# Two norms moved by token halves into their neighbour stages, the last two chunks of a feed-forward summed together, and the next seam reordered

## The chip, the cores and the metric

One NeuronCore of a Trainium2 chip runs the whole program in one launch. Its engines are TensorE (PE in the profile), VectorE (DVE), ScalarE (ACT), GpSimd (POOL) and SyncE (SP, which issues the DMAs). The metric is device time in microseconds, from launch to end. Lower is better.

## The reference

Three different transformer blocks run one after the other on x of 1024 tokens by 1024 channels, all in fp32.

```python
def layer_norm(x, g, b):                   # block 1, after each half
    mu = jnp.mean(xf, axis=-1, keepdims=True)
    var = jnp.mean(jnp.square(xf - mu), axis=-1, keepdims=True)
    y = (xf - mu) * lax.rsqrt(var + LN_EPS)
    return (y * g + b)

def rmsnorm(x, g):                         # block 2, ahead of each half and at its end
    return x * lax.rsqrt(jnp.mean(x * x, axis=-1, keepdims=True) + EPS) * g

# block 1: pool + HGRN mixer, then
h = layer_norm(ALPHA * h + mix, ln1_g, ln1_b)
u = h @ w_up                               # 1024 -> 2 x 2816
a, v = split(conv_b + causal_conv3(u, conv_w))
h = layer_norm(ALPHA * h + (gelu(a) * v) @ w_down, ln2_g, ln2_b)
# block 2: h = rmsnorm(x, norm_mix_g); proj = h @ w_in (q, k, v, ga, gb, forget logits)
#   u = ga * sigmoid(gb), causal depthwise convolution over 31 tokens; attention; w_out
#   x = x + square(relu(rmsnorm(x, norm_ffn_g) @ w_ffn_up)) @ w_ffn_down; rmsnorm(x, norm_final_g)
# block 3: modulated layer norm of x and of a context (256 tokens), projection, spatial gating,
#   mLSTM in both directions, w_out; layer norm; modulated layer norm;
#   x = layer_norm(ALPHA_3 * x + g2 * (square(relu(h @ w1 + b1)) @ w2 + b2))
```

## The kernel before

**Layout.** Channels lie on the 128 partitions, tokens along the free side: an activation is 8 tiles (KT) of 128 channels by 1024 tokens, and most instructions work on 512 tokens, a half (n = 0 or 1). X is the residual, H the input of the next product. Products are made in three passes of single-pass precision (fp32r): each operand is split into a rounded high part and a low rest, and each product is high x high, high x low and low x high, three matmuls of 128x512 with 8 tiles of input, so that a unit (128 output channels, 512 tokens) is 24 matmuls. ScalarE rounds the high part, VectorE subtracts to get the low one.

**Stages.** The program is a row of stages. Each is a block in which every engine has its own list of instructions, in the order in which the code calls them, held together by semaphores; a stage ends on all engines before the next begins. The ones that matter are, with their time in the profile: chain_stage for block 1 (467.4 to 1351.7), layer_norm_stage (to 1387.1), block2_project (to 1625.9), some stages of block 2, chain_stage for block 2 (1951.8 to 2789.2), block3_mixer (to about 3197), chain_stage for block 3.

**chain_stage** does w_out, a norm (A), an up projection, the activation and the down projection. The hidden width is taken in chunks: 22 of 128 pairs of channels in block 1 (E = 21 is the last, E-1 the one before), 16 in the others. up_unit makes one unit, down_half the 8 output tiles of one half for one chunk, and VectorE adds each from psum to X (a drain, L1688 or L1685). down_last, in blocks 2 and 3, adds the last two chunks in psum, so that only one drain per tile is needed. At the end stands the final norm, one per half (B[0], B[1]), and in block 2's chain also the first norm of block 3 for half 0 (F).

**HalfNorm** is a norm for one half, as methods that an engine's list calls: add (seven additions of the 8 tiles, for the mean), mean (a matmul with a matrix of 1/1024, which sums over partitions), centre, squares (ScalarE), pairs (four additions of two squares), sums (four matmuls), root (1/sqrt as exp of log on ScalarE), scale (VectorE), apply (ScalarE, with gain and bias) and low (VectorE). Which engine does add and pairs is set where they are called. For a centred norm whose result feeds a product ("split" or "next"), a tile goes through

```python
dve.tensor_tensor(work(k), work(k), rstd, mult)                 # scale, L944
act.activation(hi, work(k), Identity, scale=g(k), bias=b(k))    # L996: the high part, rounded
act.activation(work(k), work(k), Identity, scale=g(k), bias=b(k))   # L998: the full value
dve.tensor_tensor(HR, work(k), hi, subtract)                    # low, L955
```

**layer_norm_stage** between block 1 and block 2 is a whole stage: squares on ScalarE (L467), 16 sum matmuls (L452), root, scale with gain (L504), rounding (L487), low part (L512), for both halves, and the residual is stored to memory (spill), since its buffer is used otherwise in block 2.

**block2_project** takes 11 slabs of weights: 8 for the gates, q and k, a small one, and two for v. Units go slab by slab, in each both halves. For each of the first four slabs VectorE makes u = ga * sigmoid(gb) (gated, L2050) and 31 convolution taps (L2059, L2062), with the splits of later weight slabs (L2043) put between them.

**block3_mixer** begins with the rest of the norms of the second seam: B1 (block 2's final norm, half 1: root and scale L946), F0 and F1 (block 3's first norm), then the units for gates, q and k, the context's scaling (L3083), and rows of the gates (L2839, L2859 to L2870, L3089 on).

## Time and profile before

| | us |
|---|---|
| median of 3 runs (lowest, highest) | 4078.4 (4076.28, 4080.22) |
| profiled execution | 4078.99 |
| its span | 4077.0 |
| TensorE busy | 3735.3 (92%) |
| VectorE busy | 2271.2 (56%) |
| ScalarE busy | 1278.5 (31%) |
| GpSimd busy | 191.3 (5%) |
| mean granted clock of TensorE | 0.959 |

Of the 40 slices of the page, TensorE's busy share falls to 8 and 5 tenths in the two slices from 1223 to 1427, and below 9 in a dozen others. A matmul's length in the timeline is longer than the distance to the next, since they overlap in the array.

### The profile page before, as it was taken

Reading aid. Unit: us, or ns where it says so; the run is one execution under the profiler, and the core shown is the slowest. Engines: PE = TensorE matmul, PEld = TensorE weight load, DVE = VectorE, ACT = ScalarE, POOL = GpSimd, SP = SyncE. Lnnn points to the kernel's source line nnn. Section 1 sums busy time; section 2 is a strip of 40 time slices with the busy share of each in tenths; the row PEclk is TensorE's granted clock in tenths of the full one; section 3 lists DMA queues with packets and bytes.
Section 4 is the critical chain, followed back from the end, with each engine's and each line's share of the span. In section 5 each row is a group of like instructions: output and inputs, shape, how many; then the busy total and the mean of one; then the engine's idle time right before and its main releaser. Section 6 shows DMA issues by size and latency. Waiting matters only on the chain. (4 is left out here: it accounts for less than half of the span.)

```text
span 4077.0 us, 44926 instructions
## 1 busy us (share of the span) xinstructions
PE 3735.3 (92%) x17850; PEld 3048.8 (75%) x17850; DVE 2271.2 (56%) x3220; ACT 1278.5 (31%) x1870; POOL 191.3 (5%) x119
## 2 busy tenths in 40 slices
PE   6987899999998599688899999997898989999997
PEld 5887777888886388366778888885886757888886
DVE  1077667777777597244445645545537574444445
ACT  1142352222222421544332223224422363322323
POOL 3410000000000000000000000003001000000000
PEclk9999899999999799788999999998999999999999
DMA  2110001111110111100112222212122201111111
GB/s 106 51 63 0 21 32 57 47 47 47 47 47 21 72 47 42 62 0 0 42 52 104 93 96 97 97 42 78 36 66 65 76 28 52 42 42 62 42 52 52
DMA packets 60837, 216.56 MB, mean 53 GB/s; under 512 B 4542, under 2 KB 17086, under 8 KB 55155
## 3 DMA queue, kind: packets, MB, share of 16 engines
q1 hardware_dynamic: 60082, 213.37, 14.7%
q8 instruction: 124, 2.03, 0.2%
q10 hardware_dynamic: 576, 0.72, 0.0%
q14 instruction: 55, 0.44, 0.0%
HBM read 200.34 MB, written 13.70 MB: 52 GB/s over the span
## 5 line engine op out<-in xcount | busy, mean ns | idle before, releaser
L1250 PE MATMUL psum<-mixer_r,pairs_r 128*128 128x512 f32 x2016 | 797.9, 396 | 36.0 <-DVE gemm_input_r L1618 19.4
L1251 PE MATMUL psum<-gemm_input_r,pairs_r 128*128 128x512 f32 x2016 | 789.3, 392 | 0.0
L1252 PE MATMUL psum<-mixer_r,pairs_r 128*128 128x512 f32 x2016 | 789.1, 391 | 0.0
L1288 PE MATMUL psum<-hidden_r,pairs_r 128*128 128x512 f32 x1248 | 493.6, 396 | 20.7 <-DVE residual L1688 9.6
L1290 PE MATMUL psum<-hidden_r,pairs_r 128*128 128x512 f32 x1248 | 489.4, 392 | 0.0
L1289 PE MATMUL psum<-hidden_r,pairs_r 128*128 128x512 f32 x1248 | 489.4, 392 | 0.0
L1250 PEld LDWEIGHTS psum<-mixer_r,pairs_r 128*128 128x128 f32 x2016 | 381.3, 189 | 128.1 <-DVE pairs_r L1613 20.6
L1688 DVE TENSOR_TENSOR residual<-residual,psum 128x512 f32<-128x512 f32 x576 | 372.5, 684 | 166.9 <-PE psum L1290 146.5
L1251 PEld LDWEIGHTS psum<-gemm_input_r,pairs_r 128*128 128x128 f32 x2016 | 381.5, 189 | 80.7 <-issue 3.1
L1252 PEld LDWEIGHTS psum<-mixer_r,pairs_r 128*128 128x128 f32 x2016 | 381.1, 189 | 79.6
L1624 DVE TENSOR_TENSOR pairs_r<-pairs,pairs_r 128x2048 fp32r<-128x2048 f32 (+1 forms) x108 | 223.5, 2072 | 279.5 <-ACT pairs_r L1416 279.4
L1416 ACT ACTIVATE pairs_r<-pairs 128x2048 fp32r<-128x2048 f32 (+1 forms) x108 | 187.1, 1736 | 600.1 <-DMA pairs<-in_w 376.1
L1288 PEld LDWEIGHTS psum<-hidden_r,pairs_r 128*128 128x128 f32 x1248 | 236.3, 189 | 73.4 <-DVE residual L1688 10.9
L1685 DVE SCALAR_TENSOR_TENSOR residual<-psum,ada,residual 128x512 f32<-128x512 f32 x240 | 179.7, 751 | 177.0 <-PE psum L1290 168.0
L1290 PEld LDWEIGHTS psum<-hidden_r,pairs_r 128*128 128x128 f32 x1248 | 236.3, 189 | 49.7
L1289 PEld LDWEIGHTS psum<-hidden_r,pairs_r 128*128 128x128 f32 x1248 | 236.6, 190 | 49.1 <-issue 0.8
L1648 DVE TENSOR_TENSOR hidden_r<-mixer,hidden_r 128x512 fp32r<-128x512 f32 x172 | 118.8, 691 | 107.2 <-ACT mixer L1433 87.3
L1424 ACT ACTIVATE conv_raw<-psum 128x512 f32<-128x512 f32 x88 | 52.4, 597 | 353.9 <-PE psum L1252 353.9
L2062 DVE SCALAR_TENSOR_TENSOR mixer<-scratch,params,mixer 128x1024 f32<-128x1024 f32 x120 | 154.1, 1284 | 3.9
L1657 DVE TENSOR_SCALAR mixer<-conv_raw,params 128x512 f32<-128x512 f32 x88 | 48.1, 546 | 158.6 <-ACT conv_raw L1424 158.6
L247 PE MATMUL psum<-gemm_input_r,weights_r 128*128 128x512 f32 x256 | 100.6, 393 | 34.6 <-DVE residual_r L614 34.6
L1972 PE MATMUL psum<-residual_r,pairs_r 128*128 128x512 f32 x272 | 107.1, 394 | 23.5 <-DVE pairs_r L2043 23.5
(470 smaller groups left out, 5937.1 us busy)
## 6 DMA issues: line engine op xcount, KB each, us to landing
pairs<-in_w_up SPq DMA_DIRECT2D x38, 1024.0 KB, 7.1
pairs<-in_w SPq DMA_DIRECT2D x32, 1024.0 KB, 5.3
pairs<-in_w_down SPq DMA_DIRECT2D x16, 1024.0 KB, 5.2
norm_a<-in_w_ada SPq DMA_DIRECT2D x12, 1024.0 KB, 5.1
norm_b<-in_w_ada SPq DMA_DIRECT2D x12, 1024.0 KB, 5.0
pairs<-in_w_down SPq DMA_DIRECT2D x22, 512.0 KB, 3.3
pairs<-in_w_in SPq DMA_DIRECT2D x11, 1024.0 KB, 5.2
weight_slots<-in_w_in SPq DMA_DIRECT2D x10, 1024.0 KB, 4.8
```

Of the source, the lines that this page charges most:

```text
L1250: pe.matmul(out, w_hi[:, at], c.MR[:, k, halves[n]], start=k == 0, stop=False)
L1251: pe.matmul(out, w_hi[:, at], c.HR[:, k, halves[n]], start=False, stop=False)
L1252: mm = pe.matmul(out, w_lo[:, at], c.MR[:, k, halves[n]], start=False, stop=k == KT - 1)
L1288: pe.matmul(bank, hi, hid(0, ch, n, kd), start=kd == 0, stop=False)
L1289: pe.matmul(bank, lo, hid(0, ch, n, kd), start=False, stop=False)
L1290: mm = pe.matmul(bank, hi, hid(1, ch, n, kd), start=False, stop=kd == KD - 1)
L1416: act.activation(hi, src, ACT.Copy).then_inc(split_hi, 1)
L1624: dve.tensor_tensor(lo, src, hi.bitcast(F32), ALU.subtract).then_inc(split_ready, 1)
L1648: dve.tensor_tensor(hid(1, ch, n, m), mixed[n][:, m, :], hid(0, ch, n, m).bitcast(F32), ALU.subtract).then_inc(hid_ready, 1)
L1685: dve.scalar_tensor_tensor(out=x, in0=ps, scalar=gate(m), in1=x, op0=ALU.mult, op1=ALU.add).then_inc(down_drained, 1)
L1688: dve.tensor_tensor(x, x, ps, ALU.add).then_inc(down_drained, 1)
L2062: dve.scalar_tensor_tensor(out=out, in0=U[:, j:j + T], scalar=w, in1=out, op0=ALU.mult, op1=ALU.add).then_inc(taps, 1)
```

## The change

**First seam.** layer_norm_stage between block 1 and block 2 is gone. Its norm (norm_2) is two HalfNorms now. For half 0, its squares and three of its pair sums are at the end of block 1's chain (F), and its last pair sum, sums, root, scale, apply and low are at the start of block2_project (F0). The final norm of block 1 is split too: half 0 (B[0]) in the chain, half 1 (B1) with its adds in the chain and all else in block2_project, followed by F1. All adds and pair sums of these four are on GpSimd. block2_project takes the first three slabs for half 0 first (six units), then for half 1, and from the fourth on both halves slab by slab. Three slabs are loaded in the chain. The residual is stored in four parts, by half and by four tiles.

**Last chunks of block 1.** The order (E-1,0), (E-1,1), (E,0), (E,1) becomes (E-1,0), (E,0), (E-1,1), (E,1), and the down sums of the two chunks are one psum sum with one drain per tile.

**Second seam.** The mixer's gate slab is rounded and split in the chain before. F's sums come two tiles earlier. B[1]'s mean and sums leave the chain (norm_final is not centred, so only the sums count); B1's last pair sum and sums open the mixer. B1's root stands between F0's rounding of tiles 0 to 2 and the rest. B1's eight final scales come behind slab q's split. F1's sums come before slab k's second unit. The eight context scalings go from VectorE (L3083) to ScalarE.

**HalfNorm.** For centred norms of kind "split" or "next" (lean), the gain goes into scale and the bias into the rounding and into low. The activation L998 is gone for them. This holds for block 3's norm at the second seam and for the second norm of block 3's chain.

```diff
@@ HalfNorm @@
+        self.lean = self.centred and self.kind in ("split", "next")
...
-        if self.centred:
+        if self.centred and not self.lean:
             dve.tensor_tensor(self.work(k), self.work(k), self.rstd, ALU.mult).then_inc(self.s["scaled"], 1)
         else:
-            dve.scalar_tensor_tensor(out=self.work(k), in0=self.x(k), scalar=self.g(k), in1=self.rstd, op0=ALU.mult,
-                                     op1=ALU.mult).then_inc(self.s["scaled"], 1)
+            dve.scalar_tensor_tensor(out=self.work(k), in0=self.work(k) if self.centred else self.x(k), scalar=self.g(k),
+                                     in1=self.rstd, op0=ALU.mult, op1=ALU.mult).then_inc(self.s["scaled"], 1)
...
+        if self.lean:
+            dve.scalar_tensor_tensor(out=self.c.HR[:, k, self.half], in0=self.work(k), scalar=self.b(k),
+                                     in1=self.hi(k).bitcast(F32), op0=ALU.add, op1=ALU.subtract).then_inc(self.s["lo_ready"], 1)
+            return
...
+            if self.lean:
+                act.activation(hi, self.work(k), ACT.Identity, bias=self.b(k)).then_inc(self.s["hi_ready"], 1)
+                continue
@@ chain_stage, TensorE, block 1 @@
+                up_unit(E, 0, 0)
+                up_unit(E, 0, 1)
+                up_unit(E - 1, 1, 0)
                 down_last(0, range(0, 4))
                 down_last(0, range(4, 8))
-            up_unit(E, 1, 0)
...
+                up_unit(E - 1, 1, 1)
+                B[0].mean(pe)
+                up_unit(E, 1, 0)
+                up_unit(E, 1, 1)
                 B[0].sums(pe)
+                down_last(1, range(0, 4))
+                down_last(1, range(4, 8))
@@ chain_stage, GpSimd, block 1 @@
+                for k in range(1, KT):
+                    B[0].add(pool, k, (down_drained, down_at[E, 0, k]))
+                B[0].pairs(pool)
+                for k in range(1, KT):
+                    B[1].add(pool, k, (down_drained, down_at[E, 1, k]))
+                F.pairs(pool, range(0, 3))
@@ chain_stage, VectorE, block 1, its end @@
+                for k in range(0, 4):
+                    b0.scale(dve, k)
+                for m in range(4):
+                    drain(E, 1, m)
+                    b0.scale(dve, 4 + m)
+                drains(E, 1, range(4, 8))
+                return
@@ block2_project, TensorE @@
-            for i in range(9):
...
+            B1.mean(pe)
+            F0.sums(pe)
+            unit(0, 0, 0, F0.s["lo_ready"])
+            unit(0, 1, 0)
+            unit(1, 0, 0)
+            B1.sums(pe)
+            unit(1, 1, 0)
+            unit(2, 0, 0)
+            unit(2, 1, 0)
+            F1.sums(pe)
+            unit(0, 0, 1, F1.s["lo_ready"])
+            for u in units[7:]:
+                unit(*u)
@@ block2_project, VectorE @@
             split_slab(0)
+            B1.centre(dve, range(0, 4))
+            F0.scale_low(dve, 2)
             split_slab(1)
+            B1.centre(dve, range(4, 8))
+            split_slab(2)
+            for k in range(KT):
+                B1.scale(dve, k)
+            F1.scale_low(dve, 2)
             gated(0)
@@ block3_mixer @@
+            B1.sums(pe)
             unit("gate", 0, 0, F0.s["lo_ready"])
...
             unit("k", 0, 0)
+            F1.sums(pe)
             unit("k", 1, 0)
-            F1.sums(pe)
...
+            for k in range(KT):
+                scale, shift = [c.ada[:, 2 * (i + k) + 1:2 * (i + k) + 2] for i in (8, 0)]
+                act.activation(N[:, k, :], N[:, k, :], ACT.Identity, scale=scale, bias=shift).then_inc(ctx_step, 1)
...
-            F0.scale_low(dve, 3)
+            F0.scale_low(dve, 2)
+            split_slab("q")
             for k in range(KT):
                 B1.scale(dve, k)
-            split_slab("q")
             split_slab("k")
...
-                dve.tensor_scalar(N[:, k, :], N[:, k, :], scale, shift, ALU.mult, ALU.add).then_inc(ctx_step, 1)
@@ plan @@
-            (2, lambda f: layer_norm_stage(c, X, H, KT, ones_d, rms_eps, g("norm_mix_g_2"), centre=False,
-                                           hi=XR, lo=HR, spill=True,
-                                           prefetch=f("w_in_2"))),
-            (2, lambda f: block2_project(c)),
+            (2, lambda f: block2_project(c, final_1, norm_2)),
```

The instruction lists show where the work goes. VectorE at the end of block 1's chain and up to the first split of the projection, before (residual is X, norm_a and norm_b hold sums and squares, a branch ends a stage):

```order
L926 TENSOR_TENSOR norm_a<-norm_a,residual 128x512
L933 TENSOR_TENSOR residual<-residual,psum 128x512 x8
L938 TENSOR_TENSOR norm_a<-norm_a 128x512
L938 TENSOR_TENSOR norm_b<-norm_b 128x512 x3
L944 TENSOR_TENSOR residual<-residual,norm_a 128x512 x8
L136 UNCONDITIONAL_BRANCH
L489 UNCONDITIONAL_BRANCH
L504 SCALAR_TENSOR_TENSOR gemm_input<-residual,params,scratch 128x512 x8
L512 TENSOR_TENSOR gemm_input_r<-gemm_input,residual_r 128x512 x8
L504 SCALAR_TENSOR_TENSOR gemm_input<-residual,params,scratch 128x512 x8
L512 TENSOR_TENSOR gemm_input_r<-gemm_input,residual_r 128x512 x8
```

and now:

```order
L1756 TENSOR_TENSOR residual<-residual,psum 128x512
L955 TENSOR_TENSOR residual<-residual,norm_a 128x512
L1756 TENSOR_TENSOR residual<-residual,psum 128x512 x4
L136 UNCONDITIONAL_BRANCH
L2181 UNCONDITIONAL_BRANCH
L2208 MEMSET scratch 128x30
L2186 TENSOR_TENSOR pairs_r<-pairs,pairs_r 128x2x1024
L944 TENSOR_TENSOR residual<-residual,psum 128x512 x4
L957 SCALAR_TENSOR_TENSOR gemm_input<-residual,params,norm_a 128x512 x3
L970 TENSOR_TENSOR gemm_input_r<-gemm_input,residual_r 128x512
L957 SCALAR_TENSOR_TENSOR gemm_input<-residual,params,norm_a 128x512
```

The adds (L926), the pair sums (L938) and half 1's centre (L933) and scale (L944) have left the stage's end, and the scales and low parts of the norm between stand in the projection. GpSimd had nothing there. Its list at the end of block 1's chain and in the projection is now (L937 is add, L949 pairs):

```order
L1657 UNCONDITIONAL_BRANCH
L937 TENSOR_TENSOR norm_a<-residual 128x512
L937 TENSOR_TENSOR norm_a<-norm_a,residual 128x512 x6
L949 TENSOR_TENSOR norm_a<-norm_a 128x512
L949 TENSOR_TENSOR norm_b<-norm_b 128x512 x3
L937 TENSOR_TENSOR norm_a<-residual 128x512
L937 TENSOR_TENSOR norm_a<-norm_a,residual 128x512 x6
L949 TENSOR_TENSOR norm_a<-norm_a 128x512
L949 TENSOR_TENSOR norm_b<-norm_b 128x512 x2
```

These are B[0]'s adds and pairs, B[1]'s adds and three pairs of F. ScalarE at the start of block 3's mixer, before:

```order
L978 ACT_TABLE_LOAD
L980 ACTIVATE norm_a<-psum,rms_eps 128x512
L982 ACTIVATE norm_a<-norm_a 128x512
L2807 ACTIVATE pairs_r<-pairs 128x1024
L996 ACTIVATE residual_r<-gemm_input,ada 128x512
L998 ACTIVATE gemm_input<-gemm_input,ada 128x512
L996 ACTIVATE residual_r<-gemm_input,ada 128x512
L998 ACTIVATE gemm_input<-gemm_input,ada 128x512
```

and now:

```order
L1011 ACTIVATE residual_r<-gemm_input,ada 128x512 x3
L993 ACT_TABLE_LOAD
L995 ACTIVATE norm_a<-psum,rms_eps 128x512
L997 ACTIVATE norm_a<-norm_a 128x512
L1011 ACTIVATE residual_r<-gemm_input,ada 128x512 x3
L2958 ACTIVATE hidden_r<-mixer 128x2x1024
L1011 ACTIVATE residual_r<-gemm_input,ada 128x512 x2
L2958 ACTIVATE pairs_r<-pairs 128x2x1024
L2990 ACTIVATE rows<-psum,row_params 128x512
L3003 ACTIVATE pairs<-pairs,ada 128x256 x8
```

One activation a tile in place of two, the gate slab's rounding (L2807 with 128x1024) has left the stage, and the context's scalings (L3003) are new here.

## Rows read from the trace of the kernel before

**Rows 1.** The page: the span, and busy time of each engine with its instructions.

```profile
span 4077.0 us, 44926 instructions
...
PE 3735.3 (92%) x17850; PEld 3048.8 (75%) x17850; DVE 2271.2 (56%) x3220; ACT 1278.5 (31%) x1870; POOL 191.3 (5%) x119
```

**Rows 2.** Waits of TensorE, 1255 to 1395: total, times, longest, in us.

```profile
PE psum L1972 <- DVE pairs_r L2043: 23.5, 1, 23.5
PE psum L912 <- DVE norm_a L926: 9.9, 1, 9.9
PE psum L452 <- ACT scratch L467: 9.0, 1, 9.0
PE psum L1288 <- DVE residual L1688: 7.7, 1, 7.7
PE psum L917 <- DVE norm_a L938: 5.6, 1, 5.6
PE psum L1288 <- DVE hidden_r L1648: 3.8, 1, 3.8
```

**Rows 3.** Windows, all engines: length, busy us (instructions), granted clock, DMA share, GB/s.

```profile
1272.10:1391.92 119.82, 60.46 (x174) 36.83 (x173) 81.36 (x128) 54.92 (x84) 0.00 (x0) 0.76 0.13 53
1391.92:1625.50 233.58, 233.52 (x1200) 201.00 (x1200) 186.38 (x141) 48.60 (x65) 0.00 (x0) 0.99 0.11 39
```

**Rows 4.** Timeline, first seam and projection: start, length, engine, line, operation, [idle before].

```profile
1276.00 0.47 PE L1288 MATMUL psum<-hidden_r,pairs_r 128*128 128x512 f32 x1 [3.77 <-DVE hidden_r L1648]
...
1280.88 0.40 PE L1290 MATMUL psum<-hidden_r,pairs_r 128*128 128x512 f32 x1
...
1366.79 0.75 DVE L504 SCALAR_TENSOR_TENSOR gemm_input<-residual,params,scratch 128x512 f32<-128x512 f32 x1 [16.67 <-ACT scratch L474]
...
1372.10 0.68 DVE L512 TENSOR_TENSOR gemm_input_r<-gemm_input,residual_r 128x512 fp32r<-128x512 f32 x1
...
1391.77 0.79 PE L1972 MATMUL psum<-residual_r,pairs_r 128*128 128x512 f32 x1 [23.48 <-DVE pairs_r L2043]
...
1416.84 1.23 DVE L2050 TENSOR_TENSOR scratch<-mixer 128x1024 f32<-128x1024 f32 x1 [22.92 <-ACT mixer L2000]
...
1597.69 1.28 DVE L2062 SCALAR_TENSOR_TENSOR mixer<-scratch,params,mixer 128x1024 f32<-128x1024 f32 x1
```

**Rows 5.** Timeline, second seam.

```profile
2797.50 0.77 PE L2585 MATMUL psum<-residual_r,pairs_r 128*128 128x512 f32 x1 [8.30 <-DVE gemm_input_r L955]
...
2808.15 1.41 DVE L946 SCALAR_TENSOR_TENSOR residual<-residual,params,norm_a 128x512 f32<-128x512 f32 x2
...
2815.79 0.79 PE L2585 MATMUL psum<-residual_r,hidden_r 128*128 128x512 f32 x1 [6.54 <-DVE hidden_r L2961]
...
2845.51 1.89 ACT L2854 ACTIVATE ctx_hi<-pairs 128x2048 fp32r<-128x2048 f32 x1
...
2875.86 1.48 DVE L3089 SCALAR_TENSOR_TENSOR mixer<-mixer 36x1280 f32<-36x1280 f32 x1 [12.62 <-ACT mixer L2870]
```

**Rows 6.** Timeline, GpSimd, and VectorE beside it, second seam.

```profile
2758.79 1.54 POOL L926 TENSOR_TENSOR norm_a<-norm_a,residual 128x512 f32<-128x512 f32 x1
...
2813.45 2.29 DVE L2961 TENSOR_TENSOR hidden_r<-mixer,hidden_r 128x2048 fp32r<-128x2048 f32 x1
...
2813.61 5.46 POOL L926 TENSOR_TENSOR norm_a<-residual 128x512 f32<-128x512 f32 x1 [25.59 <-DVE residual L946]
...
2817.85 1.37 DVE L3083 TENSOR_SCALAR pairs<-pairs,ada 128x256 f32<-128x256 f32 x1
...
2819.22 1.28 POOL L926 TENSOR_TENSOR norm_a<-norm_a,residual 128x512 f32<-128x512 f32 x1
```

**Rows 7.** Timeline, second norm of the third feed-forward, half 1.

```profile
3372.58 0.81 ACT L996 ACTIVATE mixer_r<-gemm_input,ada 128x512 fp32r<-128x512 f32 x1 [0.76 <-DVE gemm_input L944]
...
3373.43 0.81 ACT L998 ACTIVATE gemm_input<-gemm_input,ada 128x512 f32<-128x512 f32 x1
...
3385.15 0.69 DVE L955 TENSOR_TENSOR gemm_input_r<-gemm_input,mixer_r 128x512 fp32r<-128x512 f32 x1 [0.86 <-ACT gemm_input L998]
```

385 lines of the change are left out of this document (241 added, 144 removed).

## The prediction, on record before the changed kernel ran

> **What bounds the kernel now.** I read the page first: TensorE is busy 92% of the span [rows 1], so only stretches in which TensorE waits or runs on other things than products can give much. The profiled execution took 4078.99 us, its span is 4077.0 and 2.0 lie around it; the median of the runs shown is 4078.4, so the sum below is made against 4079.0 and then moved by -0.6. Next the waits of TensorE from 1255 to 1395: six waits, 23.5 + 9.9 + 9.0 + 7.7 + 5.6 + 3.8 = 59.5 us, all on VectorE or ScalarE steps of a norm, a drain or a split [rows 2]. Then the windows: from 1272.10 to 1391.92, 119.8 us long, TensorE is busy 60.5 us with 174 matmuls, at a mean granted clock of 0.76; the projection behind it, 233.6 us, is dense [rows 3]. At full clock one 128x512 product follows the last after 0.227 us (816 x 0.227 and 384 half as wide at 0.127 make the 233.6); behind the wait of 3.77 us at 1276.00 the first thirteen took 4.9 us instead of 2.95, in part 0.43 apart, the 1.2 GHz level [rows 4]. By the code the 119.8 us hold five units of 24 products that are needed anyway (the chunk's down sums for half 0, its two up units for half 1, the down sums of both chunks for half 1): 120 x 0.227 = 27.2 us. The rest, 92.6 us, is seam: norm sums, waits and low clock.
>
> The second seam (second feed-forward to the third block's mixer) has waits of 8.3 and 6.5 us [rows 5], and in the third feed-forward an eight-tile norm is paced by ScalarE [rows 7].
>
> **Seam 1, part by part.** Removed: the stage between, 1351.7 to 1387.1 = 35.4 us. Its sum matmuls (16, recorded as 32; 15.5 us) and its squares, scales and roundings (L504 twice 5.4 us, L512 twice 4.9 us) [rows 4] come back as two half norms of 4 sum matmuls each, since squares are added in pairs first. Of the 16 drains of chunk E-1, 0.61 us apart on VectorE, nothing remains: both chunks add up in one psum bank, so the wait of 7.7 us for a drain and the 3.8 us for hidden_r (filled now by another unit's products) go [rows 2]. The seven adds and four pair sums of a half, now between drains on VectorE (0.69 each, one drain-and-add pair each 1.33 us), go to GpSimd, 1.29 to 1.45 us apiece when undisturbed [rows 6]: slower, but beside the products for half 0.
>
> What remains as excess over dense products, walked along the new order on each engine with the durations of before:
> - drains of half 0 of the last chunk wait for the unit before: 1.9;
> - the sums of final_1's half 0 (four, recorded as eight, 0.43 apart) and its mean on TensorE: 3.9;
> - waits of the last down sums for a drained bank, as VectorE does scale and drain in turn, 1.22 us a pair against 0.68 of products: 0.8 + 2.4 + 0.5 + 0.5 + 1.2 = 5.4;
> - the tail: GpSimd can start half 1's adds when tile 1 of it is drained, about 6.7 us before TensorE's last product, and needs seven adds at 1.38 and three pair sums at 1.30, three of these ten stretched by 0.5 beside scales: 15.1 us, so the stage ends 8.5 us after the last product: 8.5;
> - entry of the projection: last pair sum 1.3, four sums to 4.6, root 1.4, two scales, one rounding and the first low part: first product at 9.3 (this takes the place of 4.7 now: 1387.1 to 1391.8, which is in the 92.6);
> - first unit paced by scale plus low part, 1.34 a tile against TensorE's 0.68 until VectorE runs out of scales: 2.9;
> - sums of final_1's half 1 and of norm_2's half 1: 3.4 each, 6.9;
> - half 1's first unit: six units of half 0 (6 x 5.45 = 32.7 us) cover centre, squares, pairs, sums, root, scale, apply and squares again of half 1, but not all: sums of final_1 at 28.7 to 32.1, root 2.0, then scale, apply and square in turn at 1.37 a tile to 46, last pair 47, sums 48.4 to 51.9, root 1.4, two scales, rounding and low part: product at 56.4, when the six units are done at 51.9: wait 4.5, then again paced, 2.8;
> - one wait for a late split in the value part: 3.9;
> - low clock behind the four waits of over 2 us, at most 1.9 each as behind the one above: 2.0 taken (bounds 0 and 7.6).
> Sum 52.0, against 92.6: **seam 1 gives 40.6**. Where I cost at nothing: the chain of convolution taps (31 for each of four tiles) on VectorE. It starts at 1416.8 now and ends at 1606.9 [rows 4], 18.6 us before the projection's products do. In the new order VectorE first does 4.9 + 10.7 + 5.4 + 10.7 = 31.7 us for norms (centre, scale and low, final scale, scale and low); the first product of gates starts the chain at 71 of the stage, it lasts 187 to 190 us, and ends at 258 to 261, against products to 264: cover of only 3 to 6 us. If the chain takes 10 us more, 4 to 7 of that is paid.
>
> **Seam 2.** The gate slab is rounded and split in the stage before, under products; final_2's half 1 sums come first in the mixer. The first gate product comes at 4.1 instead of 8.0 after the start: -3.9. The paced unit takes 8 x 1.34 instead of 8 x 1.55 (next paragraph): -1.7. Slab q's split does not stand behind eight final scales of 5.4 us [rows 5]: -5.4. So slab q's first product is 11.0 earlier. Eight context scalings, 10.3 us on VectorE beside GpSimd's adds [rows 6], go to ScalarE, beside the products of slab q (eight activations 128x256, under 0.5 each as the 512 wide take 0.81). In half 1's norm the centre step no longer stands behind L3083 but waits for GpSimd's adds (a new wait of 6.2 on TensorE, for its mean): -7.0. Its sums come before a unit of 5.4 on TensorE: -3.7. L2854 (1.9) no longer stands ahead of its first rounding: -1.8. The pace: -2.2. So its last low part comes 14.7 earlier, and the rows that feed L3089 [rows 5] 16.2, as L3087 is done before and no longer holds the context's product. The mixer's end follows the row steps: **-17**. The chain stage before it: the added round and split (1.0 and 1.2 us) lie beside products, and F's sums move up by two down tiles: 0 (bounds -1 and +3).
>
> **Lean norms.** In the two second norms of the third feed-forward, ScalarE does L996 and L998 in turn, 12.6 us from 3372.58 to the last low part at 3385.15: 1.55 us a tile [rows 7]. After it, ScalarE does one activation (0.81) and VectorE scale plus low, each a SCALAR_TENSOR_TENSOR of 0.75 as L946 takes at 5.4 for eight [rows 5], with 0.08 overlap: 1.34 while both alternate, 0.67 for the last ones. Four scales 2.75, four pairs 5.4, three lows 2.0 put the last low at 3382.0: -3.1. Two such halves, the first partly behind sums: **-7**.
>
> Sum: 40.6 + 17 + 7 = 64.6; 4079.0 - 64.6 - 0.6 = 4013.8. **I forecast 4015**, rounding to the side of the GpSimd terms.
>
> **GpSimd beside VectorE.** What the rows show: an add of 1.29 us took 5.46 when VectorE ran two 2.29 us splits with both sources in SBUF; the next six took 8.44, and L3083 beside them 1.35 each; beside drains and splits with a psum source six adds took 8.70 [rows 6]. The unknown price of an add lies between 1.26 (no contention) and 5.46; I take 1.38, as nearly all the VectorE work beside the tail is 0.69 long, and 1.8 for those beside scales. The Trainium skill, "SBUF — State Buffer", section "SBUF: two separate sides", says that the port pair of VectorE and GpSimd is an exclusive lock held for the whole instruction, also when VectorE reads two SBUF inputs. The row of 5.46 and L3083's 1.35 agree with it. By that rule each waits for at most one instruction of the other at a time, as I have it; without it the sum would be some 7 us better.
>
> **Rivals.**
> 1. GpSimd is disturbed more. About 30 of its adds and pair sums stand on the path: 10 in the tail, 1 + 4 + 4 in the projection, 11 in the mixer. At 1.5 times 1.3 they cost 20 more (4034); at twice, 39 (4053). For: the 5.46 row. Against: 8.70 for six.
> 2. Slower than before: every one of the 30 meets a long split (2.3 us) on each side, as the one at 2813.61 did, and takes 5.46. That is 30 x 4.2 = 125 more, 4139. It decides from 65/30 = 2.2 us more per instruction, that is 3.5 us each. Against: beside the tail stand drains and scales of 0.7, not splits.
> 3. The convolution chain becomes the projection's end: it starts 71 us into the stage, now 29.7, and splits are spread otherwise. With 10 to 16 us more in it than now: 4019 to 4025. For: VectorE would be busy 218 of 264 us.
> 4. Seam 2 and the lean norms give nothing, since the mixer ends by other chains (GpSimd memsets, rows, a slab's landing): 4079.0 - 40.6 - 0.6 = 4038.
> 5. GpSimd undisturbed and the clock never low behind the waits: 7 and up to 4 better, 4004.
>
> **How the numbers follow.** Forecast with its own range 4006 to 4024 (rival 3 in part inside): 0.60. Rival 5: 0.07. Rival 1: 0.15. Rival 3 beyond: 0.06. Rival 4, or half of it: 0.06. Same: 0.02. Rival 2: 0.04. The range 4000 to 4040 leaves out the two ends (rival 1 at twice, rival 2, the same, some of the others), under 0.2. Within 0.2% (8 us) is what a measurement of this kernel can't tell from no change: 0.02. Faster 0.94, slower 0.04.
>
> **What the profile after would show.** Right: no 128x512 sums x32 between the stages; GpSimd adds at the first chain's end, ending 8 to 9 us after TensorE's last product there; a first projection product 9 us into the stage; a wait of 4 to 5 us before half 1's first unit; the first tap of the convolution near 1390; L3089 16 us earlier relative to the mixer's start; the paced units at 1.34 us a tile. Wrong: adds of over 2 us in a row, TensorE waiting for the convolution chain or for splits by more than 10 us in the projection, or the mixer's end not moved although its first rows are.

## The result, and the profile after

Four runs of the changed kernel took 4015.04 to 4018.89 us, median 4017.05. The kernel before took 4076.28, 4078.40 and 4080.22; a fourth run of it, 250 us longer, is left out of the comparison and makes its median of four 4079.31. The ratio is 0.985 (0.9833 to 0.9867): 61 us faster. Forecast: 4015, within 4000 to 4040.

The page of the kernel after, to be read against [rows 1]:

```profile
span 4017.1 us, 44871 instructions
...
PE 3728.0 (93%) x17834; PEld 3044.8 (76%) x17834; DVE 2242.4 (56%) x3174; ACT 1258.7 (31%) x1846; POOL 235.0 (6%) x149
```

The span fell by 59.9 us, TensorE's busy time by 7.3 of them only: what went was waiting. GpSimd has 43.7 us more work.

The waits of TensorE from 1225 to 1345 (total, times, longest), which stand where [rows 2] stood:

```profile
PE psum L922 <- PEq L136: 8.2, 1, 8.2
PE psum L2082 <- DVE gemm_input_r L970: 4.8, 3, 4.2
PE psum L1336 <- DVE residual L1756: 2.2, 2, 2.1
PE psum L1319 <- DVE residual L1756: 1.6, 1, 1.6
PE psum L1336 <- DVE hidden_r L1716: 0.5, 1, 0.5
```

17.3 us against 59.5. The largest one left is the end of the chain's stage, the tail of the GpSimd adds. The seam and the projection in the timeline of TensorE (start, length, operation, idle before it and its releaser), to be read against [rows 4]:

```profile
1306.12 0.47 PE L1336 MATMUL psum<-hidden_r,pairs_r 128*128 128x512 f32 x1 [2.06 <-DVE residual L1756]
...
1322.41 2.05 PE L922 MATMUL psum<-norm_a,ones_d 128*128 128x512 f32 x2 [8.25 <-PEq L136]
...
1333.91 0.47 PE L2082 MATMUL psum<-residual_r,pairs_r 128*128 128x512 f32 x1 [4.24 <-DVE gemm_input_r L970]
...
1380.87 0.76 PE L2082 MATMUL psum<-residual_r,pairs_r 128*128 128x512 f32 x1 [4.25 <-DVE gemm_input_r L970]
...
1539.87 0.58 PE L2109 MATMUL psum<-pairs_r,residual_r 128*128 128x256 f32 x1 [3.56 <-DVE pairs_r L2186]
```

In order: a last down sum waits for a drained bank; the stage ends 8.25 us after the last product; the projection's first product; half 1's first unit (F1); the late split in the value part. GpSimd at the chain's end and the projection's start (L937 the adds, L949 the pair sums):

```profile
1312.90 5.51 POOL L937 TENSOR_TENSOR norm_a<-norm_a,residual 128x512 f32<-128x512 f32 x4 [0.59 <-DVE residual L1756]
1318.36 1.26 POOL L949 TENSOR_TENSOR norm_a<-norm_a 128x512 f32<-128x512 f32 x1
1319.58 2.48 POOL L949 TENSOR_TENSOR norm_b<-norm_b 128x512 f32<-128x512 f32 x2
1325.65 2.17 POOL L949 TENSOR_TENSOR norm_b<-norm_b 128x512 f32<-128x512 f32 x1 [3.59 <-issue]
```

Half 1's last four adds take 1.38 each, the price I had taken. The last row is the first operation of the new stage: it comes 3.59 us late, and the profile names nothing that it waited for.

Where the 59.9 us went, by the first instruction of each stage in the two timelines (us; the boundaries are the same instructions in both kernels). In this table and below, chain 1 to 3 are the chain stages of blocks 1 to 3, and the mixer starts with its first load of weights:

| stretch | before | after | difference |
|---|---|---|---|
| start to block 1's chain | 470.79 | 474.04 | +3.25 |
| chain 1 to the projection's first product | 920.98 | 859.87 | -61.1 |
| that product to the convolution's norm | 234.39 | 254.37 | +20.0 |
| the convolution's norm | 25.63 | 30.36 | +4.7 |
| pointwise product | 53.63 | 52.45 | -1.2 |
| attention | 249.77 | 242.69 | -7.1 |
| chain 2 to the mixer | 834.29 | 834.23 | -0.1 |
| mixer, to slab q's first product | 26.31 | 18.76 | -7.55 |
| to the gate rows (L3089, now L3241) | 60.07 | 55.03 | -5.04 |
| to chain 3 | 324.94 | 328.99 | +4.05 |
| chain 3 to the end | 876.20 | 866.31 | -9.9 |

The second and third lines together are seam 1: -41.1. The mixer's three lines together give -8.5. Four lines moved that I had not costed: the start (+3.25, ahead of any changed code; it is 469.9 to 474.0 over all fourteen profiles, with the same code), the convolution's norm, the pointwise product and attention, whose code is the same in both.

### The profile page after: what moved, and what is told of

The parts are those of the page before. It is cut to its first block and busy times, and to the rows that moved or that the text cites. A ratio compares the mean times of both kernels' runs of the same rounds, so it can differ in the third digit from the quotient of the medians.

```text
span 4017.1 us, 44871 instructions
## 1 busy us (share of the span) xinstructions
PE 3728.0 (93%) x17834; PEld 3044.8 (76%) x17834; DVE 2242.4 (56%) x3174; ACT 1258.7 (31%) x1846; POOL 235.0 (6%) x149
## 5 line engine op out<-in xcount | busy, mean ns | idle before, releaser
L1319 PE MATMUL psum<-hidden_r,pairs_r 128*128 128x512 f32 x1216 | 478.0, 393 | 11.3 <-DVE residual L1750 6.1
L1320 PE MATMUL psum<-hidden_r,pairs_r 128*128 128x512 f32 x1216 | 474.6, 390 | 0.0
L1321 PE MATMUL psum<-hidden_r,pairs_r 128*128 128x512 f32 x1216 | 474.5, 390 | 0.0
L1756 DVE TENSOR_TENSOR residual<-residual,psum 128x512 f32<-128x512 f32 x560 | 362.2, 684 | 167.0 <-PE psum L1321 140.1
L1319 PEld LDWEIGHTS psum<-hidden_r,pairs_r 128*128 128x128 f32 x1216 | 229.2, 188 | 62.0 <-DVE residual L1750 7.7
L1321 PEld LDWEIGHTS psum<-hidden_r,pairs_r 128*128 128x128 f32 x1216 | 229.1, 188 | 48.3
L1320 PEld LDWEIGHTS psum<-hidden_r,pairs_r 128*128 128x128 f32 x1216 | 229.2, 188 | 47.5 <-issue 0.5
L2356 PE MATMUL psum<-scratch 65*128 65x512 f32 (+2 forms) x192 | 89.1, 584 | 21.7 <-DMA scratch<-rows 16.5
```

What stands on the lines that cost most here:

```text
L1319: pe.matmul(bank, hi, hid(0, ch, n, kd), start=kd == 0, stop=False)
L1320: pe.matmul(bank, lo, hid(0, ch, n, kd), start=False, stop=False)
L1321: mm = pe.matmul(bank, hi, hid(1, ch, n, kd), start=False, stop=kd == KD - 1)
L1756: dve.tensor_tensor(x, x, ps, ALU.add).then_inc(down_drained, 1)
```

## Experiments

Each result is the median, then in brackets its ratio to the kernel before, run beside it, with the 95% interval.

**The two seams apart.** The first kernel has the changed block 1 (its chain, its two norms, the new projection) and the old rest; the second has the changed rest and the old block 1, with layer_norm_stage back.

```diff
@@ first seam only: chain_stage and HalfNorm of before for blocks 2 and 3, old block3_mixer @@
@@ second seam and lean norms: chain_stage of before for block 1 @@
-            (2, lambda f: block2_project(c, final_1, norm_2)),
+            (2, lambda f: layer_norm_stage(c, X, H, KT, ones_d, rms_eps, g("norm_mix_g_2"), centre=False, hi=XR, lo=HR,
+                                           spill=True, prefetch=f("w_in_2"))),
+            (2, lambda f: block2_project(c)),
```

> The kernel before with only block 1's feed-forward and the second projection as changed (first seam and the last two chunks); second seam and lean norms as before. Forecast's account: 40.6 less, 4038. The account by stages of the two traces: 41 less up to the projection's end, 4 to 5 of it given back in the stage behind (GpSimd starts late there), so 36 less, 4043; the attention's length may move it by up to 7 either way.

> The changed kernel with block 1's feed-forward, the norm stage and the second projection put back as before; second seam and lean norms as changed. Forecast's account: 17 + 7 = 24 less, 4055. By the stages of the two traces: mixer 8.6 less (it had 15 and lost 6 at its end, where the granted clock was 0.5), third chain 9.9 less, so 18 less, 4061. If the 6 us at the mixer's end are the clock's and depend on when the stretch comes, they may be back here: 4055.

Measured: 4035.51 (0.9896, 0.988 to 0.9913) and 4056.3 (0.9947, 0.9931 to 0.9964), beside 4078.01. That is -42.5 and -21.7, together 64 against some 61 for both. The parts add up within their spread (the second kernel's four runs lie between 4049.5 and 4059.8). The first is below both accounts of it (4038 and 4043), the second between its two (4055 and 4061). In the first, chain 1 to the projection's first product is 860.37 and the mixer as before; in the second, slab q's first product comes at 18.76 instead of 26.31 and the gate rows 55.02 behind it instead of 60.07, the same as with both. But one line differs: the stretch from the rows to chain 3 is 323.48 with seam 2 alone and 328.99 with both.

**The lean norms of chain 3 alone.**

```diff
@@ before, with the changed chain_stage and HalfNorm for block 3's chain only @@
+        self.lean = self.centred and self.kind in ("split", "next")
```

> The kernel before with the third feed-forward alone as changed (lean second norms). Forecast: 7 less, 4072. By the traces' third chain: 9.9 less, 4069. Rival: the pace of the scales is hidden and nothing comes of it, 4079.

Measured: 4067.23 (0.9975, 0.9963 to 0.9986), and chain 3 took 868.67 against 876.20: -7.5, where the working has -7. In the kernel after it is 866.31, and 864.7 to 866.5 in every kernel that holds the mixer's change too. The further 2.4 us are the clock's: the first 84.45 us of chain 3, at a mean granted clock of 0.97 with the lean norms alone, are 83.45 at 0.98 in the kernel after, and a norm's stretch 120 us into the chain is 23.01 at 0.87 there and 21.57 at 0.94 here, with the same instructions. What set the clock is open.

VectorE in that norm after the change, where [rows 7] had one low part in 1.55 us:

```profile
3313.99 2.74 DVE L957 SCALAR_TENSOR_TENSOR gemm_input<-gemm_input,ada,norm_a 128x512 f32<-128x512 f32 x4 [4.06 <-ACT norm_a L997]
3316.64 0.75 DVE L967 SCALAR_TENSOR_TENSOR gemm_input_r<-gemm_input,ada,mixer_r 128x512 fp32r<-128x512 f32 x1
3317.31 0.75 DVE L957 SCALAR_TENSOR_TENSOR gemm_input<-gemm_input,ada,norm_a 128x512 f32<-128x512 f32 x1
...
3318.63 0.75 DVE L957 SCALAR_TENSOR_TENSOR gemm_input<-gemm_input,ada,norm_a 128x512 f32<-128x512 f32 x1
...
3321.95 2.73 DVE L967 SCALAR_TENSOR_TENSOR gemm_input_r<-gemm_input,ada,mixer_r 128x512 fp32r<-128x512 f32 x4
```

A scale and a low part now take 1.32 us (one L957 to the next, 3317.31 to 3318.63), where a tile took 1.55, and the last four low parts follow without a gap. All eight tiles take 10.7 us, 3313.99 to 3324.68.

**Why GpSimd starts each stage late.** The mixer of the kernel after, GpSimd, then TensorE, then ScalarE:

```profile
2752.88 2.35 POOL L949 TENSOR_TENSOR mixer<-mixer 128x512 f32<-128x512 f32 x1 [12.51 <-issue]
```

```profile
2755.29 1.22 PE L928 MATMUL psum<-mixer,ones_d 128*128 128x512 f32 x1 [2.82 <-POOL mixer L949]
...
2766.77 0.50 PE L2735 MATMUL psum<-residual_r,hidden_r 128*128 128x512 f32 x1 [1.22 <-DVE hidden_r L3118]
```

```profile
2757.40 0.69 ACT L995 ACTIVATE norm_a<-psum,rms_eps 128x512 f32<-128x512 f32 x1 [5.20 <-PE psum L928]
```

B1's last pair sum ends at 2755.2, and only then come its sums, its root and, behind the root on ScalarE, the rest of F0's rounding: VectorE waits 5.35 us for that. By the code, a stage begins on GpSimd with one semaphore clear for each semaphore of the stage before: 46 ahead of the projection's first pair sum, 34 ahead of the convolution norm's, 64 ahead of the mixer's. The experiment puts them behind GpSimd's own work in these three stages; another does each clear twice.

```diff
-    def stage(self, *names):
+    def stage(self, *names, late=False):
...
-            if retired:
+            if retired and not late:     # else the same loop behind the stage's own list
...
@@ the other kernel @@
-                    for s in retired:
+                    for s in retired * (2 if twice else 1):
                         pool.sem_clear(s)
```

> The changed kernel with GpSimd's clearing of the semaphores of the stage before moved behind its own work in three stages (projection, convolution norm, mixer). Theory: the 3.6, 2.6 and 5 us by which GpSimd's first sum comes late in these stages are the 46, 34 and 64 clears ahead of it, 0.075 us each; gone, TensorE's waits for it (about 1.1, 2.1 and 2.8 us, and the rest of those norms behind) go too: 5 to 10 less than the changed kernel, 4008 to 4012. Rival: GpSimd starts late for another reason (fetching its code): no change, 4017.

> The changed kernel with each clear of a semaphore of the stage before done twice in the projection, the convolution norm and the mixer: 46, 34 and 64 clears more ahead of GpSimd's first sum, 0.075 us each. Theory of the clears: the projection's first product 3.4 later, the convolution norm 2 to 3 longer, slab q's first product in the mixer 4.8 later, so 8 to 11 more, 4026 to 4028, the clock's outcome apart. Rival (late start for another reason): 4017.

Measured: mixer start to slab q's first product 14.76 with the clears late, 18.76 as they are, 22.20 twice; the convolution's norm 28.16, 30.36, 32.12. GpSimd and TensorE in the mixer with the clears late, then with the clears twice:

```profile
2751.23 1.26 POOL L954 TENSOR_TENSOR mixer<-mixer 128x512 f32<-128x512 f32 x1 [7.69 <-POOLq L136]
```

```profile
2771.76 1.26 POOL L949 TENSOR_TENSOR mixer<-mixer 128x512 f32<-128x512 f32 x1 [17.04 <-issue]
```

```profile
2773.07 2.08 PE L928 MATMUL psum<-mixer,ones_d 128*128 128x512 f32 x2 [6.16 <-POOL mixer L949]
```

With them twice TensorE waits 6.16 us in place of 2.82 for the same pair sum. The mechanism is shown: undoing and doubling it move the same stretch down by 4.0 and up by 3.4. The stretch up to the projection's first product stayed with the clears late (859.88 against 859.87), so there the clears were not what it waited for; with 46 more of them it is 2.4 longer (862.29). The totals do not follow, and the one with the clears late misses the 4008 to 4012 that was expected: 4018.16 (0.985, 0.9833 to 0.9866) with the clears late, no gain, and 4032.84 (0.9886, 0.987 to 0.9903) with them twice, +16 where the three stages explain 3.4 + 1.8 + 2.4 = 7.6. In both, attention took longer: 247.15 and 254.26 against 242.69. More on this below.

**Adds on VectorE.** The working assumed that adds between drains cost more than adds on GpSimd.

```diff
-                    B[0].add(pool, k, (down_drained, down_at[E, 0, k]))
-                    B[1].add(pool, k, (down_drained, down_at[E, 1, k]))
...
+                drains(E, 0, range(KT), b0)
+                    b1.add(dve, k, (down_drained, down_at[E, 1, k]))
```

> The changed kernel with the fourteen mean additions of block 1's final norm back on VectorE (half 0 between drains, half 1 behind the last drains); pair sums stay on GpSimd. By VectorE's rows: half 1's adds end about 1319 where GpSimd's last pair sum ends at 1322 now, and half 0's adds push VectorE's own list back by up to 5 us in a stretch in which TensorE has products. If GpSimd's 1.3 to 1.8 us per sum is what holds the end of the chain: up to 3 less, 4014. If moving them away from VectorE was what kept its list short: 2 to 5 more, 4019 to 4022.

Measured: 4022.11 (0.9863, 0.9846 to 0.9879) beside 4075.69, but chain 1 to the projection's first product is 858.64 against 859.87. The 5 us more sit in attention, which is 8.0 longer (250.67), against a start that is 3.1 shorter. In its own stretch the add on VectorE is 1.2 us better, the wait at the stage's end 5.6 instead of 8.2. That 14 adds went to GpSimd is not what seam 1 gained by. The eight fewer drains per half have a run of their own (9.2 us, below); the other 32 of the 41.1 us, filled waits and a norm beside products, are read from the waits (59.5 us before, 17.3 after) and not separated by a run.

**Clears late and the pair sums on VectorE too.**

```diff
-                F.pairs(pool, range(0, 3))
+                F.pairs(dve)
...
-            B1.pairs(pool, range(3, 4))
+            B1.pairs(dve, range(3, 4))
```

> The kernel with late clears, and the pair sums of the norm between (all four of half 0) on VectorE behind the last drains, and final_2's last pair sum first on VectorE in the mixer. By the stages: the chain ends 3 to 4 earlier (GpSimd has seven adds and no pair sums), the projection starts its sums without the wait for GpSimd, 1 to 2, the mixer 1 to 3 more: 5 to 9 less than with late clears alone, 4009 to 4013, if the attention stage keeps its 247 us; its length was 242.7, 247.2 or 249.8 in the kernels so far, so up to 5 either way.

Measured: 4013.54 (0.9845, 0.9829 to 0.9861). Chain 1 to the projection's first product 857.33, -2.5; the mixer's start 14.74, as with the clears late alone; the convolution's norm 26.46, close to 25.63 of before; attention 247.08. The convolution's norm has the same code as with the clears late alone, where it took 28.16: its first eight sums took 3.70 us here and 5.40 there, so the 1.7 between the two are the clock's.

**The last chunks with a drain each.** The new order is kept, but each chunk has its own down sums and eight drains per half.

```diff
-                down_last(0, range(0, 4))
-                down_last(0, range(4, 8))
+                down_half(E - 1, 0)
+                down_half(E, 0)
...
+                drains(E - 1, 0)
+                drains(E - 1, 1)
```

> The changed kernel with the last two chunks of block 1's feed-forward each summed and drained by itself again (same order of chunks and same places of the norms): sixteen more drains of 0.61 on VectorE, 9.8 us. Theory: half of them are hidden beside products, the others stand ahead of the last drains: 4 to 8 more, 4021 to 4025. Rival: VectorE has room for all of them, 4017.

Measured: 4030.04 (0.9884, 0.9868 to 0.9901), 13.0 above the kernel after, of which 4.6 are attention's (247.26); chain 1 to the projection's first product 869.09, +9.2, where 4 to 8 were expected. Waits of TensorE from 1225 to 1345 in that kernel:

```profile
PE psum L922 <- PEq L136: 10.8, 1, 10.8
PE psum L1320 <- DVE residual L1757: 8.8, 4, 5.4
PE psum L2085 <- DVE gemm_input_r L970: 4.2, 1, 4.2
PE psum L922 <- POOL norm_a L937: 1.4, 1, 1.4
```

Sixteen drains of 0.61 are 9.8 us of VectorE, and 9.2 of them are paid: at this seam VectorE's own sequence is the path, through the drained banks (8.8 against 1.6) and the tail (10.8 against 8.2).

**The late split moved.** Slab 9's split (L2186) goes in front of the last taps of the third slab, slab 10's four taps earlier.

```diff
@@ on top of clears late and pair sums on VectorE @@
-            conv(2, 12, 31)
-            gated(3)
+            conv(2, 12, 27)
             split_slab(9)
-            conv(3, 0, 16)
+            conv(2, 27, 31)
+            gated(3)
+            conv(3, 0, 12)
             split_slab(10)
-            conv(3, 16, 31)
+            conv(3, 12, 31)
```

> The version with late clears and pair sums on VectorE, and the split of the first v slab moved ahead by the last four taps of tile 2 and gated(3), that of the second by four taps. VectorE has 5.6 us in hand at the projection's end; TensorE waits 3.6 us for that split: 3 to 3.6 less than without, 4010. Rival: the taps then end later than the products, nothing gained, 4013.5.

Measured: **4002.51** (4001.73 to 4004.13), ratio 0.9817 (0.9801 to 0.9834). This is faster than both kernels of the case: 75 us less than the one before, run beside it (4077.65), and 14.5 less than the changed one, which ran at another time. The page, and TensorE's waits from 1225 to 1580:

```profile
span 4000.0 us, 44871 instructions
```

```profile
PE psum L2086 <- DVE gemm_input_r L975: 9.6, 6, 4.2
PE psum L927 <- PEq L136: 6.3, 1, 6.3
PE psum L460 <- DVE scratch L423: 2.6, 1, 2.6
PE psum L1341 <- DVE residual L1760: 2.2, 2, 2.1
```

No wait for pairs_r is left in the projection: from its first product to the convolution's norm it went from 255.56 to 249.18, 6.4 us for a wait of 3.6. The other 2.8 are the clock behind that wait. The projection in the kernel that this one is built on, then here (length, busy time of TensorE, its granted clock, DMA share, GB/s):

```profile
1330.20:1585.76 255.56, 245.87 (x1216) 0.97 0.12 40
```

```profile
1327.69:1576.87 249.18, 243.07 (x1216) 0.99 0.12 41
```

Behind the wait, at 1536.16 in the first of these kernels, 27 products of 256 columns took 5.9 us; at the 0.12 us apart of those behind them they take 3.2. Of the 11.0 against the kernel that it is built on, 3.5 more lie in attention (243.59 against 247.08), which is no merit of the edit (below), and 2.8 of the profiled difference in the start (470.04 against 472.87), ahead of any edit. Against the kernel after, the stretches whose code differs give -2.2 in chain 1, -9.1 from the projection's first product to the pointwise product, and -4.0 at the mixer's start.

**What attention's length hangs on.** Three stages with nothing in them stand between the pointwise product and attention; the same kernel ran again, and so did the one with the old block 1.

```diff
+def empty_stages(c, n):
+    for _ in range(n):
+        with c.stage("unused"):
+            pass
...
+            (2, lambda f: empty_stages(c, 3)),
```

> The changed kernel with three empty stages between the pointwise stage and the attention: nothing but their barriers, 1 to 6 us. Theory (clock): what the attention, the mixer's end and other stages with gaps on TensorE take depends on when they come, so the attention's length (242.7 now) changes to another of the values seen (up to 249.8) or the mixer's end gets its clock of 1.0 back (6 less), with unchanged instructions. Rival: all stages behind keep their lengths to 0.5 us and the time is longer by the empty stages alone.

> The kernel with three empty stages once more, to see a second profiled execution of the same program. If the clock's outcome in the attention differs between executions of one kernel, its length may be 242.7 here instead of 250.7, and the time 4015 or 4021 instead of 4029. If it belongs to the kernel: 250.7 and 4029.

> The kernel with the second seam and lean norms alone once more. Its first profile showed 243.5 for the attention and the end of the mixer at a granted clock of 1.0; its other runs were 5 to 10 slower. Theory: those outcomes vary between executions: here 249.8 or 247 and 0.5 at the mixer's end, 4056. Rival: the same as in the first profile, 4049.5.

Measured: 4028.78 (0.9873, 0.9853 to 0.9892) in the runs 4028.5, 4015.25, 4029.74 and 4029.07; 4026.97 in the repeat; 4056.78 for the old block 1 again. The empty stages themselves cost 2.0 us: ahead of attention's first product TensorE is idle for 18.46 us in place of 16.48 (18.36 in the repeat), so a stage boundary is worth about 0.7. The other 8 us are attention: 250.75, and 250.83 in the repeat. For the old block 1 the low clock at the mixer's end that was expected did not come: it is 1.00 in both executions. Windows over attention (length, busy time of TensorE, its granted clock, DMA share, GB/s) of the kernel before, of after, and of the kernel with the old block 1 in its two executions:

```profile
1705.42:1955.19 249.77, 202.19 (x1088) 0.83 0.01 2
```

```profile
1671.09:1913.78 242.69, 195.17 (x1089) 0.85 0.01 2
```

```profile
1706.68:1950.13 243.45, 196.63 (x1088) 0.84 0.01 2
```

```profile
1707.36:1957.10 249.74, 202.18 (x1089) 0.83 0.01 2
```

The last two are the same program: 243.45 us once and 249.74 the other time, with as many matmuls and 5.6 us more busy time at the lower mean clock. So attention's 242.69 in the kernel after is an outcome that an unchanged program can get or miss; one run of 4015.25 among three of 4029 looks the same. It is 242.74 in the kernel with the first seam only, too, but 247.1 to 254.3 in seven of the ten profiles in which block 1 is changed. The length goes with the granted clock: what was not granted, (1 - 0.85) x 242.69, (1 - 0.83) x 249.77 and, with the clears twice, (1 - 0.81) x 254.26, is 36, 42 and 48 us of full clock, steps of 6 where the lengths differ by 7.1 and 4.5, as near as two decimals allow. The change in front of it did not earn the 7.1 us by any mechanism that the traces show. What decides how long the clock is low stays open.

## Why the prediction was right

**Seam 1: right, in its sum and in most terms.** Forecast -40.6, measured -41.1. By terms: the tail 8.25 us (forecast 8.5); half 1's first unit 4.25 (4.5); the late split 3.56 (3.9); the first half-0 drain 1.6 (1.9). Two terms were off against each other. The entry of the projection is 11.9 us long, not 9.3. Its first pair sum starts 3.6 late behind 46 semaphore clears and takes 2.17 us, but it is not what counts: with the clears late it ends 1.3 us behind TensorE's first instruction of the stage in place of 5.4, and the entry is no shorter. TensorE itself is the path. Its list has B1's mean ahead of F0's sums, 1.84 us that the working of the entry leaves out, and the two stand at a mean granted clock of 0.62; the row at 1322.41 above is the mean, the last sums and the root behind them are

```profile
1325.95 3.71 PE L928 MATMUL psum<-norm_b,ones_d 128*128 128x512 f32 x6
```

```profile
1329.71 0.69 ACT L995 ACTIVATE norm_a<-psum,rms_eps 128x512 f32<-128x512 f32 x1 [4.11 <-PE psum L928]
```

The sums end 7.6 us behind GpSimd's last operation of the chain, where the working has 4.6, and the rest of the entry took 4.2 in place of 4.7: that is the 2.6. The last down sums wait 2.7 us in all (2.2 + 0.5), not 5.4. Rival 3, the convolution chain as the projection's end, did not come: its first step (gated) and the last taps of VectorE,

```profile
1395.54 1.23 DVE L2193 TENSOR_TENSOR scratch<-mixer 128x1024 f32<-128x1024 f32 x1 [7.29 <-ACT mixer L2124]
...
1562.48 19.78 DVE L2205 SCALAR_TENSOR_TENSOR mixer<-scratch,params,mixer 128x1024 f32<-128x1024 f32 x15
```

end at 1582.2, some 5.6 us before the projection's products, within the 3 to 6 that I had.

**Behind seam 1: a term I did not have.** The convolution's norm grew by 4.7 us though its code is the same. Before, GpSimd cleared 8 semaphores there; now it clears 34 ahead of its two sums, and TensorE waits for them and then runs at the lower clock. VectorE and GpSimd before, then GpSimd and TensorE after:

```profile
1626.16 2.37 DVE L410 TENSOR_TENSOR scratch<-mixer 128x512 f32<-128x512 f32 x2 [19.27 <-PEq L136]
```

```profile
1626.72 2.93 POOL L410 TENSOR_TENSOR scratch<-mixer 128x512 f32<-128x512 f32 x2 [1214.48 <-SPq L136]
```

```profile
1590.97 2.48 POOL L418 TENSOR_TENSOR scratch<-mixer 128x512 f32<-128x512 f32 x2 [219.49 <-issue]
```

```profile
1592.28 5.45 PE L455 MATMUL psum<-scratch,ones_half 128*128 128x512 f32 x6 [2.13 <-POOL scratch L418]
```

VectorE begins the stage at 1588.28, GpSimd at 1590.97, 2.7 us later; before it was 0.6 (1626.72 after 1626.16). Six sums in 5.45 us are about 0.9 apart; before, eight took 3.97, about half of that each, the two levels of the clock. With the clears late the stage is 2.2 shorter. In the kernel that has the pair sums on VectorE as well 3.9 of the 4.7 are gone; the further 1.7 are the clock's, as said there.

**Seam 2: the path right, two prices along it missing.** Forecast -17, measured -8.5 (-14.1 with the old block 1). The terms put at nothing are GpSimd's clears ahead of the entry and the clock at the mixer's end; they are of different kinds. First, the entry: slab q's first product was to come 11.0 earlier and came 7.55, as B1's last pair sum stood behind 64 clears. With the clears late it is 11.55, and the gate rows come 16.3 us earlier than before (70.07 from the mixer's start against 86.38), where the working has 16.2. The path was drawn rightly; a price in front of it, 64 instructions that no engine counts as busy, was missing. Second, the mixer's end. With the old block 1 it follows the row steps as forecast: rows 12.6 earlier, the end 14.1. With both seams changed the rows are 12.6 earlier and the end only 8.5, since from the rows to chain 3 it took 328.99, +4.05. The windows from 24 to 4 us ahead of chain 3's first product, of before, of the kernel with the old block 1, and of after (columns as above):

```profile
3176.80:3196.80 20.00, 18.71 (x99) 1.00 0.64 257
```

```profile
3157.51:3177.51 20.00, 18.71 (x99) 1.00 0.64 259
```

```profile
3126.79:3146.79 20.00, 18.96 (x75) 0.66 0.65 262
```

In these 20 us TensorE is granted the full 2.4 GHz in before and in the kernels with only one seam changed; in all nine profiles with both seams changed (eight kernels) it falls to 1.2 GHz for a part of it: 75 matmuls in place of 99. It is reproducible, and it is worth more than the 4 us: the same products, from the last unit that waits for pairs_r (at 3071.32 in the kernel after) to chain 3, take 79.47 us at a granted clock of 0.87, against 73.51 at 0.94 before and 73.90 at 0.94 with the old block 1, which has the same mixer. So the clock costs 5.6 to 6.0; ahead of these products 1.9 were gained. With the clears late the mixer takes 399.3 us against 411.3 before, -12.0; an estimate without the 5.6 of the clock is -17.6, where the forecast has -17. Why the clock falls is not found: the work on both sides of it is the same, and both seams apart don't show it. With the lean norms alone, whose code up to chain 3 is that of before, these 20 us are at 0.91, so the clock there can differ without any change ahead of it.

**Chain stage before it: 0, measured -0.1. Lean norms: -7, measured -9.9,** of which 7.5 are the norms alone and 2.4 the clock.

**The contention of GpSimd: right in the tail, larger elsewhere.** Rival 1 needed some 2 us apiece, rival 2 over 3.5. Half 1's adds in the tail took 1.67, twice 1.63 and four times 1.38, the pair sums 1.26. But the first pair sum of the projection took 2.17, the first of B1's and of F1's 2.36 and 2.35, the mixer's first 2.35 and three of F1's there 1.94 each. The 31 operations on the path took 49.8 us, 1.61 apiece: a quarter above 1.3, half of what rival 1 has. The longest in the second seam:

```profile
2772.10 3.27 POOL L937 TENSOR_TENSOR norm_a<-residual 128x512 f32<-128x512 f32 x1 [16.87 <-DVE residual L957]
```

It is the first add of half 1 of block 3's norm, and a VectorE split of 2.29 us began 0.17 earlier:

```profile
2771.93 2.29 DVE L3118 TENSOR_TENSOR pairs_r<-pairs,pairs_r 128x2048 fp32r<-128x2048 f32 x1
```

What [rows 6] showed at 5.46, beside two such splits, is 3.27 beside one: the 2.12 that were left of the split and 1.15 more. The other six took 8.33, 1.39 each. By the rule of the Trainium skill ("SBUF — State Buffer", "SBUF: two separate sides"), whichever of the two engines starts first keeps the port pair that they share for the whole of its instruction. The trace agrees: the add ends 1.15 us behind the split, not sooner. What the prediction made of the rule, that each waits for at most one instruction of the other at a time, does not hold. In [rows 6] a second split followed the first without a gap,

```profile
2815.65 2.29 DVE L2961 TENSOR_TENSOR pairs_r<-pairs,pairs_r 128x2048 fp32r<-128x2048 f32 x1
```

and the add of 2813.61 ended at 2819.07, 1.13 behind the second: it waited for both.

**The total was partly right by cancellation.** Forecast 64.6 less in all; the changed parts gave 41.1 + 8.5 + 9.9 = 59.5, with 4.7 back in the convolution's norm: 54.8. Attention (-7.1) and the pointwise product (-1.2), against the start (+3.25), gave the other 5.1. Had attention come out at 250, as it did in six of the other thirteen profiles, the same program would have stood near 4025, still inside the range. On the other side, the low clock at the mixer's end took 5.6 us that had nothing to do with the path. So the mechanism was right to within some 10 us, and that the time came within 2 is luck.

## What to carry to other kernels

Count what an engine does before its first useful instruction: clears and other bookkeeping, which no busy time shows, stand in front of work that is moved to an idle engine, and the first operation of a stage is just the one that others wait for. Moving drains away (one psum sum for two chunks) paid 9.2 us here; moving the adds to GpSimd paid nothing. That filling a norm's waits with other units pays is read from the waits and not from a run of its own. And after a change, lay the stages side by side, the unchanged ones too: here two of them moved by 5 and 7 us, one by a cause of the change and one by none that was found.

## What the runs showed of the hardware

A semaphore clear on GpSimd takes 0.06 to 0.08 us. In the convolution's norm 26 more of them put its first sum 2.1 us later behind the stage's start (0.082 each), and 34 more on top of those another 2.1 (0.062). In the mixer the pair sum starts 4.9 us behind the start with 64 clears (0.077 each), 9.4 with 128, and at once with the clears late. That the clears twice cost slab q 3.4 and not 4.5 is the pair sum itself: it took 2.35 beside VectorE's work in the one and 1.26 in the other. The profile counts none of these instructions as busy; its "issue" in brackets is all that is seen of them.

In these rows, a GpSimd operation that meets a VectorE instruction with two tensors in SBUF ends 1.1 us behind the end of the last of VectorE's instructions that follow each other without a gap: 1.15 at 2772.10 (one split), 1.13 at 1325.65 (one split), 1.11 at 2752.88 (two instructions of 0.75), 1.13 in [rows 6] (two splits). Undisturbed the same sum takes 1.26.

One program has more than one length. Attention took 243.45 and 249.74 us in two executions of one kernel, at a mean granted clock of 0.84 and 0.83, with the same matmuls. Over all profiles it is 242.7 to 243.6, 247.1 to 247.3, 249.7 to 250.8, and once 254.3. The four runs of the kernel with three empty stages lie 14.5 us apart. So a difference of some 10 us of this kernel can't be read from the total alone; it is read from the stretch on which the edit acts.

At the mixer's end the granted clock is 1.00 before and with one seam changed, 0.91 with the lean norms alone, and 0.66 over the same 20 us with both seams changed. Nothing in the rows ahead of it that I read tells why.
